# w_down's product in a decoder block on one core: 42 products of quadrants by Strassen's scheme among w_up's units, in place of 24 plain units behind them

## The reference, cut to what matters

```python
# x: (512, 1024) after the first residual, float32
u = rms_norm(x, g_ffn) @ w_up                       # (512, 6144)
u = conv_b + sum(conv_w[j] * shift_right(u, j) for j in range(3))
gate, val = split(u, 2)
g = gelu(gate) * val                                # (512, 3072)
x = x + g @ w_down                                  # (512, 1024)
ple_gate = sigmoid(rms_norm(x, g_ple) @ w_ple_gate)
x = x + ple_gate * (p @ w_ple)
out = rms_norm(x, g_final)
```

## Time and profile before

| what | value |
|---|---|
| median of 3 runs | 950.5 us (950.4 to 950.9) |
| the profiled execution | 951.2 us |
| its span in the trace | 949.3 us |
| PE | 935.2 us busy (99%), 6,809 matmuls |
| DVE | 415.6 us (44%) |
| ACT | 428.5 us (45%) |
| POOL | 386.4 us (41%) |
| mean granted clock of PE | 0.997 |

### The profile page before, as it was taken

The page is one execution under the profiler, slowest core; times in us unless marked ns, Lnnn a source line. Parts: engine busy times, 40 slices in busy tenths (PEclk is TensorE's granted clock), DMA queues, the critical chain, the costliest instruction groups (busy, mean ns, idle before and its releaser), DMA issues.

```text
span 949.3 us, 15952 instructions
## 1 busy us (share of the span) xinstructions
PE 935.2 (99%) x6809; PEld 771.0 (81%) x6809; DVE 415.6 (44%) x640; ACT 428.5 (45%) x681; POOL 386.4 (41%) x180
## 2 busy tenths in 40 slices
PE   8999999999999999999999999999999999999996
PEld 6887888887778788888898888888888888888885
DVE  4124798308565447659344344343344300100435
ACT  6365553235555644634344444433434412412657
POOL 3442444442213526346424444444444444445350
PEclk9999999999999999999999999999999999999998
DMA  8542333332120000225412333333333333323132
GB/s 251 134 107 65 92 89 89 89 91 66 46 67 26 26 26 25 69 89 202 131 45 67 110 91 92 107 90 96 104 89 103 106 101 109 91 89 126 60 104 89
DMA packets 115163, 86.59 MB, mean 91 GB/s; under 512 B 2852, under 2 KB 100022, under 8 KB 115094
## 3 DMA queue, kind: packets, MB, share of 16 engines
q1 hardware_dynamic: 114904, 85.50, 30.5%
q10 hardware_dynamic: 190, 0.08, 0.0%
HBM read 83.47 MB, written 2.10 MB: 90 GB/s over the span
## 4 chain that ended last, share of the span: by engine, by line
PE 94%; SPq 2%; ACT 1%; DMA 1%; DVE 1%; POOL 1%; issue 0%; DVEq 0%
PE bank L545 19%; PE bank L546 18%; PE bank L547 18%; PE bank L610 9%; PE bank L612 9%; PE bank L611 9%; PE bank L883 2%; PE bank L754 1%; PE bank L791 1%; PE bank L839 1%; DMA raw<-in_w_in_dram 1%; PE bank L768 1%; PE bank L880 1%; SPq L441 1%; SPq L427 1%; PE bank L850 1%
## 5 line engine op out<-in xcount | busy, mean ns | idle before, releaser
L525 POOL TENSOR_TENSOR w_lo<-raw,w_hi 128x1024 fp32r<-128x1024 f32 x137 | 331.5, 2420 | 485.6 <-ACT w_hi L1164 474.5
L1164 ACT ACTIVATE w_hi<-raw 128x1024 fp32r<-128x1024 f32 x136 | 144.4, 1062 | 339.0 <-issue 194.5
L545 PE MATMUL bank<-hT_hi,w_hi 128*128 128x512 f32 (+1 forms) x720 | 282.1, 392 | 0.5 <-POOL w_lo L525 0.3
L546 PE MATMUL bank<-hT_lo,w_hi 128*128 128x512 f32 (+1 forms) x720 | 277.1, 385 | 0.0
L547 PE MATMUL bank<-hT_hi,w_lo 128*128 128x512 f32 (+1 forms) x720 | 277.0, 385 | 0.0
L545 PEld LDWEIGHTS bank<-hT_hi,w_hi 128*128 128x128 f32 x720 | 135.2, 188 | 28.5 <-issue 1.0
L547 PEld LDWEIGHTS bank<-hT_hi,w_lo 128*128 128x128 f32 x720 | 135.2, 188 | 27.3
L546 PEld LDWEIGHTS bank<-hT_lo,w_hi 128*128 128x128 f32 x720 | 135.3, 188 | 25.5 <-issue 0.3
L2062 DVE SCALAR_TENSOR_TENSOR cbuf<-bank,params,cbuf 128x511 f32<-128x511 f32 x48 | 36.0, 750 | 132.5 <-ACT cbuf L1564 132.5
L610 PE MATMUL bank<-w_hi,g_hi 128*128 128x512 f32 x184 | 71.7, 389 | 0.0
L612 PE MATMUL bank<-w_hi,g_lo 128*128 128x512 f32 x184 | 71.6, 389 | 0.0
(11 more groups left out here) (321 smaller groups left out, 1359.6 us busy)
## 6 DMA issues: line engine op xcount, KB each, us to landing
raw<-in_w_up_dram SPq DMA_DIRECT2D x48, 512.0 KB, 3.8
raw<-in_w_in_dram SPq DMA_DIRECT2D x33, 512.0 KB, 4.0
raw<-in_w_down_dram SPq DMA_DIRECT2D x24, 512.0 KB, 3.7
raw<-in_w_gate_dram SPq DMA_DIRECT2D x16, 512.0 KB, 4.0
raw<-in_w_out_dram SPq DMA_DIRECT2D x8, 512.0 KB, 4.2
raw<-in_w_ple_gate_dram SPq DMA_DIRECT2D x8, 512.0 KB, 4.6
xs<-in_x_dram SPq DMA_DIRECT2D x4, 512.0 KB, 5.4
raw<-in_w_branch_a_dram SPq DMA_DIRECT2D x4, 512.0 KB, 3.6
```

The lines of the kernel that those rows point to most:

```text
L525: nc.gpsimd.tensor_tensor(low(n)[:, :], raw[:, n % RAW_SLOTS, :], high(n)[:, :].bitcast(F32), ALU.subtract).then_inc(*step("pool", ("lo", n)))
L545: nc.tensor.matmul(o, wh, ah, start=first, stop=False)
L546: nc.tensor.matmul(o, wh, al, start=False, stop=False)
L1164: nc.scalar.activation(high(u)[:, :], raw[:, u % RAW_SLOTS, :], ACT.Copy) \
```

## The change

The 3,072 features of g are cut into six blocks of four tiles, and in a block the product g @ w_down becomes one of 2 x 2 quadrants: rows of the output by token halves, columns by halves of 512, features by even and odd tiles. It's done by Strassen's scheme in Winograd's form with seven products instead of eight. DVE forms the sums of g's quadrants (`mix`, in the buffer `G`) and the differences of w_down's (`difference`). Three of the products take a quadrant of w_down as it was loaded (numbers 1, 2 and 3), four a difference. A product is a unit of 12 matmuls: two banks (token tiles j), two feature tiles p, three terms. Products 6, 7 and 4 go on accumulating in the banks of product 1, and 3 in those of 5 (`CONTINUES`), and after every product DVE adds both its banks to a quadrant of `xr` (`added`); PE continues in a bank only after that addition. Product 2 takes the banks that 5 and 3 had, in a ring of two.

The products of a block stand among w_up's units of the next block, one behind each of the first seven; the last three of the fifth block and all of the sixth stand behind w_up. The four quadrants of a block have one buffer each, loaded by SP (`quadrant`), the differences two buffers of two. The split of a product's weights goes to the extra slot "up", behind w_up also to the two others in turn. The mixed tiles are kept for two blocks instead of g for all 24. p is loaded with the first block's quadrants. The norm behind w_down works on the token tiles in the order 0, 1, 2, 3 (`squares_c`, `rms_scaled_c`), and product 4, the last, completes the tiles 2 and 3.

```diff
...
+NBLOCK = NF // 4
+PRODUCTS = [(1, 5, 6, 3, 7, 2, 4)] * (NBLOCK - 1) + [(1, 5, 6, 3, 2, 7, 4)]
+CONTINUES = {6: 1, 7: 6, 4: 7, 3: 5}
+QUADRANT = {1: (0, 0), 2: (0, 0), 6: (0, 1), 3: (0, 1), 5: (1, 1), 7: (1, 1), 4: (1, 0)}
+MIXED_A = {7: 0, 1: 1, 2: 2, 4: 3, 5: 4, 6: 5, 3: 6}
+DOWN_AMONG_UP = [0] + [7] * (NBLOCK - 2) + [4]
+DOWN_BEHIND_UP = [(NBLOCK - 2, x) for x in range(4, 7)] + [(NBLOCK - 1, x) for x in range(7)]
...
+    for k in range(2 * NF):
+        t, x = divmod(k, 8)
+        if t and x == 1:
+            u.append((("dn", t - 1, 0), None, 0, 0, 0, 0))
+        u.append((("up", up_tile(k)), "w_up", 0, 8, P * up_tile(k), P))
+        if t and 2 <= x <= DOWN_AMONG_UP[t]:
+            u.append((("dn", t - 1, x - 1), None, 0, 0, 0, 0))
+    for t, x in DOWN_BEHIND_UP:
+        u.append((("dn", t, x), None, 0, 0, 0, 0))
...
-EXTRA = {("down", 1, NF // 2 - 1): "down", ("up", 1): "up", **{(name, 1, s): f"{name}{s}" for name in ("out", "pleg") for s in (1, 2, 3)}}
+RAW_UNITS = [n for n, x in enumerate(UNITS) if x[1]]
+RAW_TURN = {n: r for r, n in enumerate(RAW_UNITS)}
+EXTRA = {("up", 1): "up", **{("dn", t, x): "up" for t in range(NBLOCK - 1) for x in range(DOWN_AMONG_UP[t + 1])},
+         **{("dn", *tx): "up" for tx in DOWN_BEHIND_UP[::3]}, **{(name, 1, s): f"{name}{s}" for name in ("out", "pleg") for s in (1, 2, 3)}}
...
+        mixed_hi = at("mixed_hi", 0, [P, 2, 2, 7, SEQ // 2], F32R)
+        mixed_lo = at("mixed_lo", 28, [P, 2, 2, 7, SEQ // 2], F32R)
+        quads = at("quads", 56, [P, 4, UNIT])
+        weights_mixed = [at("mixed_w0", 72, [P, 2, UNIT]), sb_at("mixed_w1", [P, 2, UNIT], F32, yb_at)]
+        G = at("G", 88, [P, 8, SEQ // 2])
+        cbuf = at("cbuf", 96, [P, 2, 3, SEQ])
...
+        def down_bank(t, prod, j):
+            return {5: ("dy", t, 5, j), 3: ("dy", t, 5, j), 2: ("dy", t, 2, j)}.get(prod, ("dx", t, 1, j))
...
+        X_RING, UP_RING, DOWN_RING, TAIL_RING = range(0, 2), range(4, 8), range(2, 4), range(0, 4)
+        TAIL_X, TAIL_Y = range(4, 6), range(6, 8)
...
+                if label == ("up", up_tile(4)):
+                    sp.wait_ge(*done("act", "sq", "nb", 1, NT - 1))
+                    for x in range(4):
+                        quadrant(x, 0)
+                    sp.dma_start(p_raw[:, :, :], p_d).then_inc(p_in, 16)
+                for t in range(1, NBLOCK):
+                    if label == (("up", up_tile(8 * t + 8)) if t < NBLOCK - 1 else ("ple", 0)):
+                        sp.wait_ge(*done("dve", "mixed_w", 7, t - 1))
+                        sp.wait_ge(*low_of(1, t - 1))
+                        quadrant(0, t)
+                        quadrant(1, t)
+                        sp.wait_ge(*low_of(3, t - 1))
+                        quadrant(3, t)
+                    if label == (("up", up_tile(8 * t + 9)) if t < NBLOCK - 1 else ("pleg", 1, 1)):
+                        sp.wait_ge(*done("dve", "mixed_w", 4, t - 1))
+                        sp.wait_ge(*low_of(2, t - 1))
+                        quadrant(2, t)
+                r = RAW_TURN[n]
+                if r >= RAW_SLOTS:
+                    sp.wait_ge(*done("pool", "lo", RAW_UNITS[r - RAW_SLOTS]))
+                src = W[name][r0:r0 + kts * P, c0:c0 + w].rearrange("(t p) n -> p t n", p=P)
+                dst = raw[:, r % RAW_SLOTS, :].rearrange("p (t n) -> p t n", t=kts)
+                sp.dma_start(dst, src).then_inc(landed[r % RAW_SLOTS], 16)
...
+            def down_unit(t, x):
+                n, prod = UIDX[("dn", t, x)], PRODUCTS[t][x]
+                pe.wait_ge(*done("pool", "lo", n))
+                pe.wait_ge(*done("dve", "mixed_lo", 4 * t + (2 if prod in (1, 7) else 3)))
+                for j in range(2):
+                    if prod in CONTINUES:
+                        pe.wait_ge(*done("dve", "added", t, CONTINUES[prod], j))
+                        o = bank[turn[down_bank(t, prod, j)]]
+                    else:
+                        o = begin(*down_bank(t, prod, j))
+                    for p in range(2):
+                        a = slice(P * j, P * j + P)
+                        ah, al = mixed_hi[:, t % 2, p, MIXED_A[prod], a], mixed_lo[:, t % 2, p, MIXED_A[prod], a]
+                        c = slice(512 * p, 512 * p + 512)
+                        nc.tensor.matmul(o[:, :], ah, high(n)[:, c], start=p == 0 and prod not in CONTINUES, stop=False,
+                                         skip_group_check=True)
+                        nc.tensor.matmul(o[:, :], ah, low(n)[:, c], start=False, stop=False, skip_group_check=True)
+                        mm = nc.tensor.matmul(o[:, :], al, high(n)[:, c], start=False, stop=p == 1, skip_group_check=True)
+                    mm.then_inc(*step("pe", ("dn", t, prod, j), *([("unit", n)] if j else [])))
+            for k in range(2, 2 * NF):
+                t, x = divmod(k, 8)
+                feature_unit(("up", up_tile(k)), "up", up_tile(k))
+                if t and x < DOWN_AMONG_UP[t]:
+                    down_unit(t - 1, x)
+            for t, x in DOWN_BEHIND_UP:
+                if (t, x) == (NBLOCK - 1, 0):
+                    ring.update(np=TAIL_RING, dx=TAIL_X, dy=TAIL_Y)
+                down_unit(t, x)
+                if (t, x) == (NBLOCK - 1, 2):
...
+                    if UNITS[u][0][0] == "dn":
+                        t, prod = UNITS[u][0][1], PRODUCTS[UNITS[u][0][1]][UNITS[u][0][2]]
+                        if prod <= 3:
+                            act.wait_ge(quad_in[(0, 2, 3)[prod - 1]], 16 * (t + 1))
+                        else:
+                            act.wait_ge(*done("dve", "mixed_w", prod, t))
+                    else:
+                        r = RAW_TURN[u]
+                        act.wait_ge(landed[r % RAW_SLOTS], 16 * (r // RAW_SLOTS + 1))
...
+            def mixed_split(i):
+                t, p = i // 4, i // 2 % 2
+                act.wait_ge(*done("dve", "mix", i))
+                if t >= 2:
+                    act.wait_ge(*done("pe", "unit", UIDX[("dn", t - 2, 6)]))
+                of_s, of_g = (slice(2, 7), slice(3, 8)) if i % 2 else (slice(0, 2), slice(0, 2))
+                nc.scalar.activation(mixed_hi[:, t % 2, p, of_s, :], G[:, of_g, :], ACT.Copy).then_inc(*step("act", ("mixed_hi", i)))
+            for k in range(2 * NF):
+                i, z, u = k // 2, k % 2, up_tile(k)
+                t, x = divmod(k, 8)
+                if z == 0 and i:
+                    mixed_split(i - 1)
+                if k + 2 < 2 * NF:
+                    hi_upto(UIDX[("up", up_tile(k + 3 if k < 2 else k + 2))])
+                else:
+                    hi_upto(UIDX[("dn", *DOWN_BEHIND_UP[k + 3 - 2 * NF])])
+                act.wait_ge(*done("pe", "up", u))
+                if i >= 2:
+                    act.wait_ge(*done("dve", "mix", i - 2))
+                nc.scalar.activation(cbuf[:, i % 2, z, :], psum(("up", u))[:, :], ACT.Identity,
+                    scale=par("conv_w0", u), bias=par("conv_b", u)).then_inc(*step("act", ("tap0", u)))
+                if z:
+                    act.wait_ge(*done("dve", "taps", i))
+                    nc.scalar.activation(cbuf[:, i % 2, 2, :], cbuf[:, i % 2, 0, :], ACT.Gelu_apprx_tanh) \
+                        .then_inc(*step("act", ("gelu", i)))
+                if t and x + 1 < DOWN_AMONG_UP[t]:
+                    hi_upto(UIDX[("dn", t - 1, x + 1)])
+            def squares_c(h, *tiles):
+                for m in tiles:
                     act.wait_ge(*previous("act"))
+                    squares_of("nc", xr, G_junk, m, h)
+                    if h == 0:
                         root("nc", m, m + 1)
+            last = NBLOCK - 1
+            hi_upto(UIDX[("dn", last, 0)])
+            mixed_split(NF - 1)
+            hi_upto(UIDX[("dn", last, 3)])
+            bring(ACT.Sqrt)
+            hi_upto(UIDX[("dn", last, 4)])
+            gained_hi("np", None, 2, pT_hi)
+            hi_upto(UIDX[("dn", last, 6)])
+            squares_c(1, 0, 1)
+            hi_upto(UIDX[("ple", 0)])
+            squares_c(0, 0, 1)
+            hi_upto(UIDX[("ple", 1)])
+            squares_c(1, 2, 3)
+            squares_c(0, 2, 3)
...
+            def mixed_rest(i):
+                t, p = i // 4, i // 2 % 2
+                dve.wait_ge(*done("act", "mixed_hi", i))
+                of_s, of_g = (slice(2, 7), slice(3, 8)) if i % 2 else (slice(0, 2), slice(0, 2))
+                V.tensor_tensor(mixed_lo[:, t % 2, p, of_s, :], G[:, of_g, :], mixed_hi[:, t % 2, p, of_s, :].bitcast(F32),
+                                ALU.subtract).then_inc(*step("dve", ("mixed_lo", i)))
+            def mix(dst, a, b, op, *label):
+                dve.wait_ge(*previous("dve"))
+                V.tensor_tensor(G[:, dst, :], G[:, a, :], G[:, b, :], op).then_inc(*step("dve", *label))
+            def multiplied(i):
                 dve.wait_ge(*done("act", "gelu", i))
                 dve.wait_ge(*previous("dve"))
+                g = G[:, 3:5, :] if i % 2 else G[:, 1:3, :]
```

(128 more changed lines are left out.)

104 lines of the change are left out of this document (33 added, 71 removed).

## The result

The kernel with the change takes 955.9 us (median of 14 runs, 952.2 to 958.2) against 951.0 us for the kernel before beside it (14 runs): ratio 1.0049, 95% interval 1.0039 to 1.0058. It is 4.9 us slower. The sign is the forecast's (+2.2 us), and the time lies just inside its own range (949.5 to 956). Its runs spread over 6 us, those of before over 2.

The account below looks back on a forecast made before the run. PE bounds the kernel (94% of the chain that ended last). -16.3 for fewer matmuls, +9.8 blocks, +7.3 behind w_up, +1.4 norm give +2.2 us: 952.7 from a median of 950.5, own range 949.5 to 956.

Parts of the forecast that it names:

- The count: On PE: 576 matmuls become 504, and 72 fewer at 0.2267 us each save 16.3 us.
- The blocks: At each block's start, PE waits 1.96 us at the second product, in five blocks: 9.8 us.
- The rule of the turn: DVE two-tensor operations don't run beside POOL's subtraction; whoever waits gets the turn next, so the difference ends at 11.69.
- VectorE wins the turn: At block starts: waits 0.9 each, 4.5 in all; rival with DVE's way in the tail too, 944 us, chance 0.28.
- Behind w_up: Behind the last w_up unit: ten products follow each other and every collision counts, 7.3 us (bounds 0.5 and 9.5).
- The fifth of these products needs it: Behind the last w_up unit: the fifth product needs the last mixed rest, ending at 14.6, due 10.6.
- the 4.0 nor the 3.1: Behind w_up: PE waits 4.0 us at the fifth product for the last rest, 3.1 at the eighth for an addition.
- The norm: Before PLE: four token tiles are normed there, tile 3 scaled 6.8 us after the ple unit starts: 1.4 us.
- At nothing: Loads of quadrants and p, queued ahead of the fifth w_up load, cost 0; without cover up to 4 us once.
- The clock: TensorE's clock could fall after waits of 2 to 4 us; taken as 0, since DVE sets the tail's pace.
- The rival that added 8 us of this to the forecast: Clock falls at the five block waits and in the tail: 961 us, some of them 957 to 961; chance 0.12.
- nearly all is covered: Rival: DVE and POOL collisions miss, as today's do; -15.8 us, 935 us; chance 0.12.

Follow-up runs that it names:

- both experiments on the order: Each against the changed kernel: DVE's weight difference put ahead of the mixed tile's rest, 945.3 us; POOL made to wait until that difference is written, 950.0 us.
- the additions first: Changed kernel with DVE doing the fifth product's two additions before the last pair's product and mixes, and last rest before the sixth's additions: 954.6 us.
- the four edits: Changed kernel with difference ahead of rest, fifth product's additions first behind w_up, other banks for the first ple unit and for w_up's first unit: 940.1 us, 0.9882.

## Why the prediction was right, and where it wasn't

*The count* (-16.3) held: 72 matmuls, the same 0.2267 us.

*The blocks* (9.8): 5 waits of 1.88, 10.2 with what was lost just behind each. The rule of the turn from the earlier trace rows held in all five, both experiments on the order took the lost turn away, and the case "VectorE wins the turn" (0.9 each, 4.5 in all) was met when POOL was held back: PE's first matmul came 1.20 us behind the one before it in place of 2.11, so 1.20 - 0.23 = 0.97 each, 4.9 in all. The Trainium skill ("SBUF — State Buffer", Who interferes with whom) says that issue order decides which of the two engines blocks the other; the rows agree (POOL ready at 801.51, the difference issued at 801.92).

*Behind w_up* (7.3): 5.3, and by another wait. The step that failed is to let PE run until "The fifth of these products needs it": the third needs an addition already, since product 4 goes on in the banks of product 7 (`CONTINUES`). By the forecast's own times DVE starts that addition at 8.5 and takes 0.62, with PE due at 5.2, which is a wait of 3.9; 3.8 was measured. The walk noted where DVE added and not who waited. Behind this wait neither the 4.0 nor the 3.1 appeared. With the additions first a wait of 3.0 stood where the forecast had 4.0, at the fifth, but for the low part of that unit's weights (PE starts at 862.42) and not for the mixed low part (done at 860.15); the 3.1 at the eighth product never came.

*The norm* (1.4): the end chain came near its size (1.05 once nothing stood before it), but the first ple unit itself wants a bank of the last product, whose reader stands behind two scalings in DVE's order: 2.4 us, a dependence that the forecast lacked.

*At nothing*: the loads indeed cost nothing. The ring of w_up's banks, which the text passed over, cost 1.1.

*The clock*, taken as 0: nothing behind the five (a mean of 1.00 from 540 to 858 us), but 1.5 and 1.7 us behind the two longest waits. Its ground for the tail, that DVE sets the pace there, failed: those slow matmuls stayed in the time. The two falls agree with the Trainium skill ("TensorE: Matmul & The Clock Gate", What's actually happening), by which activity releases the clock; each cost lies in the 1 to 3 us that the prediction worked out beside it. The rival that added 8 us of this to the forecast was right for the tail alone, with 3.2.

In sum -16.3 + 10.2 + 5.3 + 2.5 + 1.7 + 1.1 = +4.5 us, the difference of the spans, against +2.2. That the two are so near is in part luck: 3.5 us of waits too many behind w_up (7.3 against 3.8) stood against 5.8 us too few (the clock 3.2, the norm 1.1, the ring 1.1, the blocks 0.4). The sign rested on the blocks, the term that was reasoned rightly; without their lost turns the kernel is at 945.

Of the 16.3 us the four edits keep 11 (940.1); the rival "nearly all is covered" had 935.

## What to carry to other kernels

Fewer matmuls help only as far as the two helpers that share something stay out of each other's way: before adding VectorE work on two SBUF tensors beside GpSimd work, write down for each such operation whether the other engine is already waiting when it's issued, since an operation issued directly behind another lost its turn at all five block starts here. Put what doesn't depend on the engine's last result ahead of what does; one such swap gave 10.6 us here. For each product that accumulates on in a bank, or takes a bank over, list the reader it waits for and what stands ahead of that reader on its own engine.
